# Scratch of the hidden combinations laid out by tile, and the next down groups' weights placed elsewhere in SyncE's order

## The reference

```python
def finish(x, attn_o, ret_o, gr, w_out, norm2_g, w_up, w_down, final_norm_g):
    ...
    x = x + mixed
    u = rmsnorm(x, norm2_g) @ w_up
    x = x + jnp.square(jax.nn.relu(u)) @ w_down
    return rmsnorm(x, final_norm_g)
```

## Time and profile before

| | us |
|---|---|
| median of 3 runs | 2437.24 (2435.69 to 2438.1) |
| the profiled execution | 2442.01 |
| its span in the trace | 2440.2 |
| PE busy | 2332.0 (96%) |
| DVE busy | 1554.7 (64%) |
| ACT busy | 936.7 (38%) |
| POOL busy | 894.5 (37%) |
| DMA queue q1, share of 16 engines | 47.2% |

### The profile page before, as it was taken

One profiled execution on the slowest core, in us unless ns is written; L12 is line 12 of the kernel. 1 busy time (PEld: TensorE's weight loads), 2 busy tenths in 40 slices (PEclk: granted clock), 3 DMA queues, 4 the chain that ended last, 5 costly groups with the idle time before them and its releaser, 6 DMA issues.

```text
span 2440.2 us, 45969 instructions
## 1 busy us (share of the span) xinstructions
PE 2332.0 (96%) x18396; PEld 2252.9 (92%) x18396; DVE 1554.7 (64%) x2316; ACT 936.7 (38%) x1213; POOL 894.5 (37%) x357
## 2 busy tenths in 40 slices
PE   8999999999999999889999999998889999999997
PEld 8979899999999899889999899998889999999997
DVE  5358625555555533397777687776667777777775
ACT  5241222222222322255555555555433333333344
POOL 2413323333222544244344344434333333333354
PEclk9999989999999999899999999999999999999998
DMA  6523323333333443317777666676875455545532
GB/s 216 139 67 101 80 69 87 88 90 87 89 91 90 140 126 109 121 43 188 196 196 192 167 186 177 193 195 186 286 280 192 174 217 201 191 174 218 200 123 79
DMA packets 345430, 368.76 MB, mean 151 GB/s; under 512 B 15730, under 2 KB 300594, under 8 KB 336818
## 3 DMA queue, kind: packets, MB, share of 16 engines
q1 hardware_dynamic: 333218, 352.15, 47.2%
q10 hardware_dynamic: 12064, 14.53, 1.6%
HBM read 288.85 MB, written 77.80 MB: 150 GB/s over the span
## 4 chain that ended last, share of the span: by engine, by line
PE 73%; DMA 12%; DVE 6%; POOL 3%; ACT 2%; issue 2%; SPq 1%; ACTq 0%; DVEq 0%; POOLq 0%
PE product L917 36%; PE product L628 29%; DMA raw<-in_w_up_dram 9%; PE banks L659 6%; POOL w_lo L588 3%; DMA raw<-in_w_down_dram 1%; PE banks L656 1%; ACT w_hi L1216 1%; DVE banks L1800 1%; DVE h_lo L1836 1%; DVE s_up L1749 1%; DMA x_in<-in_x_prompt_dram 1%; DMA w_raw<-in_w_in_dram 1%; DVE a_lo L1407 0%; DMA hidden_combinations<-h_lo 0%
## 5 line engine op out<-in xcount | busy, mean ns | idle before, releaser
L588 POOL TENSOR_TENSOR w_lo<-raw,w_hi 128x1024 fp32r<-128x1024 f32 x193 | 523.3, 2713 | 838.5 <-ACT w_hi L1216 838.2
L917 PE MATMUL product<-s_up,w_hi 128*128 128x260 f32 x3600 | 658.7, 285 | 48.7 <-POOL w_lo L588 32.2
L917 PE MATMUL product<-s_dn,w_hi 128*128 128x260 f32 x3584 | 654.5, 284 | 16.2 <-DVE xr L1876 14.5
L917 PEld LDWEIGHTS product<-s_up,w_hi 128*128 128x128 f32 x3600 | 558.5, 190 | 56.7 <-POOL w_lo L588 38.6
L917 PEld LDWEIGHTS product<-s_dn,w_hi 128*128 128x128 f32 x3584 | 554.4, 189 | 20.0 <-issue 15.0
L555 POOL TENSOR_TENSOR w_lo<-w_raw,w_hi 128x1024 fp32r<-128x1024 f32 (+1 forms) x134 | 324.0, 2420 | 663.9 <-ACT w_hi L1049 663.8
L917 PE MATMUL product<-s_up,w_lo 128*128 128x260 f32 x1800 | 510.6, 284 | 0.0
L917 PE MATMUL product<-s_dn,w_lo 128*128 128x260 f32 x1792 | 507.8, 283 | 0.0
L628 PE MATMUL product<-a_hi,w_hi 128*128 128x260 f32 (+1 forms) x2144 | 440.5, 287 | 7.1 <-POOL a_lo L578 2.1
L628 PE MATMUL product<-a_hi,w_lo 128*128 128x260 f32 (+1 forms) x2144 | 434.2, 284 | 0.0
L628 PE MATMUL product<-a_lo,w_hi 128*128 128x260 f32 (+1 forms) x2144 | 433.5, 284 | 0.0
(11 more groups left out here) (270 smaller groups left out, 1871.5 us busy)
## 6 DMA issues: line engine op xcount, KB each, us to landing
raw<-in_w_up_dram SPq DMA_DIRECT2D x64, 1024.0 KB, 12.1
raw<-in_w_down_dram SPq DMA_DIRECT2D x64, 1024.0 KB, 5.3
s_dn<-hidden_combinations SPq DMA_DIRECT2D x56, 1040.0 KB, 9.3
w_raw<-in_w_in_dram SPq DMA_DIRECT2D x100, 512.0 KB, 3.9
hidden_combinations<-h_hi SPq DMA_DIRECT2D x32, 910.0 KB, 6.3
hidden_combinations<-h_lo SPq DMA_DIRECT2D x32, 910.0 KB, 11.4
w_raw<-in_w_out_dram SPq DMA_DIRECT2D x32, 512.0 KB, 4.0
x_transposed<-xr ACTq DMA_DIRECT2D x2, 2080.0 KB, 7.8
```

The source lines that it names most:

```text
L588: nc.gpsimd.tensor_tensor(ring(w_lo, g, n), block_of(g, i, j), ring(w_hi, g, n).bitcast(F32), ALU.subtract).then_inc(s_lo, 1)
L917: mm_last = nc.tensor.matmul(out, w[:, k, col:col + P], s[:, h, k, :], start=(first and k == 0 and part == 0), stop=(last and k == kn - 1 ...
```

## The change

The scratch is laid out anew. Before, a partition held, for a chunk and a combination, high and low of the four tiles side by side, so that a load read 8320 contiguous bytes per partition, and a store wrote seven pieces of 1040 bytes. Now a partition holds, for a tile and for high or low, the seven combinations side by side: a store writes 7280 contiguous bytes per partition, and a load reads four pieces of 1040 bytes, in two DMAs for a position (high and low, 520 KB each). The bytes are the same. The semaphore of a position counts to 32 instead of 16 for each chunk.

SP's order changes at the change of halves and in the down half: the load of (33, 0) goes between the chunk-0 loads of positions 3 and 4; the load of (34, 0) goes right behind the last store, ahead of the wait for that store's landing and of `reload_x(2)`; `reload_x(3)` goes between the two loads of group 35; and the loads of a next chunk are spread 2, 3, 2 over three rounds, where they were 3, 2, 2.

```diff
-        h_dram = nc.dram_tensor("hidden_combinations", (P, NCHUNK, 7, 2, 4, HALF_COLS), F32).ap()
+        h_dram = nc.dram_tensor("hidden_combinations", (P, UPG, 2, 7, HALF_COLS), F32).ap()
...
             def store_hidden(g):
 
                 sp.wait_ge(s_hl, g + 1)
-                c, k = divmod(g, 4)
                 for n, x in enumerate((h_hi, h_lo)):
-                    sp.dma_start(h_dram[:, c, :, n, k, :], x[:, :, :].bitcast(F32)).then_inc(s_store, 16)
+                    sp.dma_start(h_dram[:, g, n, :, :], x[:, :, :].bitcast(F32)).then_inc(s_store, 16)
...
                 if c >= 1:
-                    sp.wait_ge(s_sd[pos], 16 * c)
-                sp.dma_start(s_dn[:, c % 2, pos, :, :, :].bitcast(F32), h_dram[:, c, pos_stored(pos), :, :, :]
-                             ).then_inc(s_sd[pos], 16)
+                    sp.wait_ge(s_sd[pos], 32 * c)
+                for n in range(2):
+                    sp.dma_start(s_dn[:, c % 2, pos, n, :, :].bitcast(F32),
+                                 h_dram[:, 4 * c:4 * c + 4, n, pos_stored(pos), :]).then_inc(s_sd[pos], 16)
...
                 if g == UPG - 1:
-                    for pos in range(7):
+                    for pos in range(4):
+                        load_hidden(0, pos)
+                    half_free(UPG + 1, 0)
+                    load_half(UPG + 1, 0)
+                    for pos in range(4, 7):
                         load_hidden(0, pos)
                 store_hidden(g - 1)
...
-            half_free(UPG + 1, 0)
-            load_half(UPG + 1, 0)
             half_free(UPG + 1, 1)
             load_half(UPG + 1, 1)
             sp.wait_ge(s_hl, UPG)
             sp.wait_ge(s_hh, UPG)
             reload_x(1, 5, 8)
             store_hidden(UPG - 1)
-            sp.wait_ge(s_store, 32 * UPG)
-            reload_x(2, 8, 12)
             for g in range(UPG + 2, GROUPS):
                 half_free(g, 0)
                 load_half(g, 0)
+                if g == UPG + 2:
+                    sp.wait_ge(s_store, 32 * UPG)
+                    reload_x(2, 8, 12)
+                elif g == UPG + 3:
+                    reload_x(3, 12, KT)
                 half_free(g, 1)
                 load_half(g, 1)
                 c, w = divmod(g - UPG - 2, 4)
-                if g == UPG + 2:
-                    reload_x(3, 12, KT)
                 if c + 1 < NCHUNK and w < 3:
-                    for pos in ((0, 1, 2), (3, 4), (5, 6))[w]:
+                    for pos in ((0, 1), (2, 3, 4), (5, 6))[w]:
                         load_hidden(c + 1, pos)
...
-                        pe.wait_ge(s_sd[pos], 16 * (c + 1))
+                        pe.wait_ge(s_sd[pos], 32 * (c + 1))
```

## The result

The changed kernel takes 2399.04 us in the median (2397.58 to 2400.01, 4 runs) against 2437.67 for the kernel before (2435.69 to 2438.86) on the same chip: a ratio of 0.9842, 95% interval 0.9825 to 0.9859, 38.6 us less. 41 were forecast. The sum came out nearly right, but of its two terms the first was under-rated (36.9 us for 34) and the second did not come (0.6 us for 7).

The account below looks back on a forecast made before the run. PE was taken to bound the down half, with stalls behind scratch stores costing the up half and the change of halves 55.5 us. Terms 34 + 7 = 41 us off the 2437.2 median gave 2396 us, range 2389 to 2421.

Parts of the forecast that it names:

- the two stretches: Up half and change of halves: 37.8 and 17.7 us lost, 55.5 us in all that changed MLP DMAs can give back.
- The stores, 34 us: Up half: each pair of scratch stores costs the queue 3.1 us less, nearly all stalls go; gain 34 us, bounds 22 to 38.
- The 4 us I held back: Up half: 4 of the 37.8 us left for rounds where something else joins the queue, such as the `xr` reload.
- The lower bound of 22: Up half: the stores' gain if each pair takes only 1.5 us less, 22 us.
- The rule against it: Scratch stores: by the 512-byte rule 1040-byte pieces lose nothing, the stores' term is zero; rival at 2432 us, chance 0.05.
- The loads, nothing in the down half: Down half: scratch loads in 1040-byte pieces take 3.0 to 3.3 us a position instead of 2.6, at no cost to PE.
- The change of halves, 7 us: Change of halves: loss falls from 17.7 to 10 to 12 us, a 7 us stall before group 33 stays; gain 7.
- -4 to +10: Change of halves: bounds of the 7 us gain, -4 if a position takes 4.4 us.
- The slower one: Stores stay at 7.7 us a pair, bound by direction to HBM, and positions go to 3.7; +5, 2442 us, chance 0.05.
- The next link: Up half: ACT's and POOL's own order holds PE almost as long, leaving about 15 of 34 us; 2415 us, chance 0.08.
- What would show it: Signs: w_up landing at 9 us or less, `h_lo` near 6, one stall of about 7 us before group 33, down half busy.
- the rest of the up half's signs: Up half: PE's wait for POOL's `w_lo` under 6 us, 5160 matmuls in about 630 us.

Follow-up runs that it names:

- pad320: The whole change with each combination padded to 320 columns in the scratch, so a store is seven 1040-byte pieces at 1280-byte steps; 2403.69 us, one run.
- loads_long: The whole change, but each scratch load reads one run of 8320 bytes per partition in one DMA (outputs wrong); 2394.97 us.
- dve_part: The whole change, with DVE making `h_lo` of tile 31 and position 6's add ahead of group 33's second sum; change of halves 85.80 us against 89.8.
- the padding to 264: The whole change with each combination padded to 264 columns in the scratch, pieces 1056 bytes apart; 2455.00 us, ratio 1.0106 to the kernel before.

## Why the prediction was right, and where it was wrong

**The reading of what bounds.** Right: only the two stretches could give anything, and 411.60 us of the down half show that it gave nothing.

**The stores, 34 us.** The effect was right and a little under-rated: 36.9 us. The landings fell about as forecast: `h_lo` lands 4.6 us earlier in the median and the following loads 2.6, where I had each pair 3.1 us shorter. All of PE's waits for POOL but one went, and that one was behind the reload that I had named. The 4 us I held back were too many: 626.5 us against 625.7 without any stall. The reason given was too simple, though. I wrote that 7280-byte pieces are "nearer to 16640 than to 1040 in what a piece must pay once", as if size were all. `pad320` shows that 1040-byte pieces pay little at 1280-byte steps. That the unbroken row helps mostly since it has one start where seven were is an inference from it. The lower bound of 22 has no working from its 1.5 us; it was not needed on that chip, and on chip B the total gain was 28.

**The rule against it.** The Trainium skill, "DMA: Bandwidth & Descriptors", Specifications, puts the least transfer for line rate at 512 bytes. I set it against 242 GB/s and gave it 0.05. The layout's gain does not agree with it, but `pad320` nearly does: 1040-byte pieces at round places land in 8.0 us, near the 6.8 of the unbroken run. The same page of the Trainium skill, "How a descriptor splits into AXI transactions", counts extra work for a descriptor that starts off a 256-byte boundary, and describes it for reads. 1280 is a multiple of 256, 1056 and 8320 are not, and the 8.0 us against 11.5 and 10.7 go the same way, though these are stores, of which it says nothing. The loads from the scratch are reads and start off such places too; the down half shows no loss that PE would feel, and `loads_long` puts it at 4 us at most.

**The loads, nothing in the down half.** Right, to 0.1 us. The landing that I gave there, within 13 us with "two loads of 3", counts one of the two; with both it is 15.9, still inside the 22.6. At the change of halves I had them at 3.0 to 3.3 us a position for 2.6; `loads_long` confirms the size, 3.6 us over seven. The issues I had at 0.4 us each "which nobody waits for". The fourteen took 1.4 us each in the median, and the chain goes through the last of them and the store's, 4.2 us, before the load of (33, 1); whether PE would gain if they were shorter is not shown.

**The change of halves, 7 us.** Wrong: 0.6. The step that failed is "position 0 of group 33 needs 41 + 1.7 + 1.0 + 2.4 = 46". I followed ACT and POOL behind the store of tile 30 and left out DVE, which stood before the same gate with a longer way: the load of (33, 1) landed at t = 44.9 (t = 0 at 1682.07), then came a sum, two adds, a `w_lo`, `h_lo` in 3.26 us and the add, and PE went on at 52.2. The store of tile 30 landed at 42.4, near the 41 of the forecast, and the wait that I computed exists, 7.4 us in `dve_part`, under the longer one. The load of (33, 0) was in time and helped nobody, as written. The stalls behind it (3.0 and 1.9 us before) did go, and most of that was given back: 11.2 us before group 33 and 2.5 in two waits inside group 32, instead of 8.1 and 1.5. That the sum came out near 41 owes something to luck: the first term made up 2.9 of the 6.4 us that the second lacked. The bounds of that term, -4 to +10, hold it.

**The rivals.** None came. The slower one, stores bound by their direction, put a pair at 7.7 us, and `h_lo`, the pair's second half, lands in 6.8. The next link (ACT and POOL) did not bind in the up half.

**What would show it.** w_up's median was to be 9 us or less and is 9.5; `h_lo` near 6 and is 6.8; the rest of the up half's signs are there. The stall before group 33 was to be 7 us and is 11.2.

## What to carry to other kernels

Where a store to a scratch is a strided pattern, look at how the pieces are placed. Here it paid to make the store one unbroken row and to have the short pieces on the load, whose landing PE waited for nowhere in the steady part. If pieces are needed, padding them to a round step may give most of it back (here 46.7 us between steps of 1056 and 1280 bytes in the up half). When a forecast says that PE goes on after a wait, follow every engine that PE waits for across the gate, the one that empties its banks too: here the order on that engine decided, and DVE's other order gave 4 us where the moved DMAs of the change gave none. Before a new order of DMAs is credited, run it alone.

## What was not expected of the hardware

- Stores of seven 1040-byte pieces per partition took 11.5 us to land at 1056-byte steps, 8.0 at 1280-byte steps, and 6.8 as one run of 7280 bytes, all behind an equal store. The closest packing was the slowest, slower than pieces 8320 bytes apart (10.7, on the same chip as the padding to 264).
- The kernel with the short stores took 2437.7, 2428.9 and 2427.1 us on three chips, the one with unbroken rows 2399.04 and 2399.06 on two. That it is the stores' cost which differs is likely (`h_lo` 11.4 and 10.7 us to landing) and not shown.
- The same 232 matmuls at 286 us ran at a mean granted clock of 0.75 or 0.86 in different executions, 4.9 us apart, with no difference in the code: behind the same pause of PE the time at 1.2 GHz was longer in one.
- SP's issues of 520 KB loads from the scratch took 1.4 us each in the median of fourteen behind each other, where seven issues of 1040 KB loads took 0.6 at the same place before.
